# Layer norm's fold, its root from PSUM, the rounding of weights and the first maxima: an order changed in four places

## The reference, cut to what matters

```
# layer 0
p = rmsnorm(x, g_mix[0]) @ w_in_a            # 12 tiles of channels, and 2 of memory queries
v = a * sigmoid(gate)                        # u = p[:1536] + b_glu, split in two halves
v = causal_dwconv(v, w_dw_a, b_dw_a)         # 31 taps, 768 channels
v = silu(layernorm(v, ln_g, ln_b))           # over the 768 channels
x = x + concat(v, memory_attention(q, mem_k, mem_v)) @ w_out[0]
x = x + conv_ffn(rmsnorm(x, g_ffn[0]), ...)  # 5632 wide, 3 taps, silu(gate) * val
# layer 1
kvf = rmsnorm(x, g_kv) @ w_kvf               # keys, values, 12 forget gates
cum_logf = cumsum(log_sigmoid(f_logit + b_f))
q, q_mem = rmsnorm(x, g_mix[1]) @ w_in_b
x = x + concat(forgetting_attention(q, k, v, cum_logf), memory_attention(...)) @ w_out[1]
x = x + conv_ffn(rmsnorm(x, g_ffn[1]), ...)
```

## Time and profile before

| | us |
|---|---|
| median of 3 runs | 1698.44 |
| lowest and highest run | 1695.33, 1699.03 |
| profiled execution, its own time | 1693.87 |
| span of the profiled execution | 1692.0 |

### The profile page before, as it was taken

How to read it: one execution, slowest core, us unless ns; L and a number is a source line. 1 busy time by engine, 2 the same in 40 slices (tenths; PEclk the granted TensorE clock), 3 DMA queues, 4 the chain that set the end, 5 groups by cost and what they waited for, 6 DMA issues and landing times.

```text
span 1692.0 us, 23831 instructions
## 1 busy us (share of the span) xinstructions
PE 1647.4 (97%) x8600; PEld 1273.5 (75%) x8600; DVE 849.4 (50%) x1408; ACT 734.5 (43%) x1165; POOL 706.7 (42%) x406
## 2 busy tenths in 40 slices
PE   7899899999999999999999999999999999999998
PEld 7655678888888876666788888888876668876666
DVE  7787545555531125433466666511355554566454
ACT  6433434444432335444445555433335643525541
POOL 4433244444455444443444444545434432434332
PEclk9999999999999999999999999999999999999999
DMA  7112132233333332110223233333321112321111
GB/s 255 60 51 64 51 100 81 93 99 99 99 111 100 100 99 75 51 50 26 100 88 92 94 99 99 112 104 107 131 63 52 62 62 63 119 63 63 51 50 62
DMA packets 40250, 143.76 MB, mean 85 GB/s; under 512 B 4592, under 2 KB 4592, under 8 KB 40176
## 3 DMA queue, kind: packets, MB, share of 16 engines
q1 hardware_dynamic: 39168, 139.59, 25.9%
q10 hardware_dynamic: 1008, 3.15, 0.6%
HBM read 140.62 MB, written 2.10 MB: 84 GB/s over the span
## 4 chain that ended last, share of the span: by engine, by line
PE 88%; DVE 6%; ACT 2%; issue 1%; DMA 1%; SPq 0%; POOL 0%; DVEq 0%; ACTq 0%; POOLq 0%
PE banks L1715 23%; PE banks L1717 23%; PE banks L1716 23%; PE banks L1893 3%; PE banks L1911 3%; PE banks L1928 3%; PE banks L1761 2%; PE banks L1763 2%; PE banks L1762 2%; DVE chain L1381 1%; PE banks L1981 1%; DVE xs_lo L1176 1%; DMA raw<-wstream 1%; ACT prob L726 1%; DVE banks L1381 1%
## 5 line engine op out<-in xcount | busy, mean ns | idle before, releaser
L581 POOL TENSOR_TENSOR w_lo<-raw,w_hi 128x1024 fp32r<-128x1024 f32 x252 | 610.2, 2430 | 733.1 <-ACT w_hi L664 732.8
L1715 PE MATMUL banks<-xs_hi,w_hi 128*128 128x512 f32 (+2 forms) x1488 | 597.4, 401 | 11.3 <-DVE xs_lo L1432 4.7
L1717 PE MATMUL banks<-xs_hi,w_lo 128*128 128x512 f32 (+2 forms) x1488 | 577.9, 388 | 0.0
L1716 PE MATMUL banks<-xs_lo,w_hi 128*128 128x512 f32 (+2 forms) x1488 | 577.0, 388 | 0.0
L664 ACT ACTIVATE w_hi<-raw 128x1024 fp32r<-128x1024 f32 x255 | 264.0, 1053 | 287.6 <-PE banks L1717 247.2
L1715 PEld LDWEIGHTS banks<-xs_hi,w_hi 128*128 128x128 f32 x1488 | 280.3, 188 | 83.7 <-issue 18.3
L1717 PEld LDWEIGHTS banks<-xs_hi,w_lo 128*128 128x128 f32 x1488 | 279.8, 188 | 58.5
L1716 PEld LDWEIGHTS banks<-xs_lo,w_hi 128*128 128x128 f32 x1488 | 280.6, 189 | 53.6 <-issue 2.9
L591 POOL TENSOR_SCALAR prob<-prob,rinv 128x512 f32<-128x512 f32 (+3 forms) x144 | 89.3, 632 | 194.4 <-DVE rinv L1230 194.1
L1715 PE MATMUL banks<-hid_hi,w_hi 128*128 128x512 f32 x352 | 136.9, 389 | 0.0
L1716 PE MATMUL banks<-hid_lo,w_hi 128*128 128x512 f32 x352 | 136.9, 389 | 0.0
(11 more groups left out here) (258 smaller groups left out, 1935.6 us busy)
## 6 DMA issues: line engine op xcount, KB each, us to landing
raw<-wstream SPq DMA_DIRECT2D x255, 512.0 KB, 3.5
x<-xT SPq DMA_DIRECT2D x4, 512.0 KB, 10.2
out<-pt SPq DMA_DIRECT2D x8, 256.0 KB, 2.1
memx<-memT SPq DMA_DIRECT2D x2, 512.0 KB, 5.9
ws_sb<-wsT ACTq DMA_DIRECT2D x2, 512.0 KB, 4.5
qk<-post_rows ACTq DMA_DIRECT2D x2, 512.0 KB, 3.5
sb_sb<-sbT ACTq DMA_DIRECT2D x2, 256.0 KB, 5.0
rope_sb<-rope ACTq DMA_DIRECT2D x1, 512.0 KB, 6.5
```

The lines of the kernel that those rows point to most:

```text
L581: nc.gpsimd.tensor_tensor(w_lo[s][:].rearrange("p k c -> p (k c)"), raw[s][:], w_hi[s][:].rearrange("p k c -> p (k c)").bitcast(f32), SUB) ...
L1715: MM(dst, w_hi[slot][:, k, :], hi, start=start, stop=False)
L1716: MM(dst, w_hi[slot][:, k, :], lo, start=False, stop=False)
L1717: return MM(dst, w_lo[slot][:, k, :], hi, start=False, stop=stop)
```

## The change

It moves work in four places and drops one copy; no arithmetic is changed.

- **First attention blocks.** DVE's maxima of blocks 0 and 4 go ahead of the gate product of units 2 and 4; ACT's exponentials of block 0 go ahead of the first sigmoid.
- **Layer norm.** DVE takes five of the last tile's seven taps, finishes tile 4, and then takes the other two. PE's fold of the last tile goes ahead of the second memory unit, the last tile's sums into its middle, the total to step 1 of the third unit; ACT copies the sums down ahead of rounding a weight unit. The transposes that spread the root go ahead of the fourth output part, and DVE multiplies by the root in PSUM, without `spread`; the last product signals `cast_down` in its place.
- **Rounding of weights.** In `residual` the unit that was rounded ahead of the splits of x is rounded behind them, once DVE has written all low parts. At unit 8 of layer 1 the rounding waits for the low parts too.
- **Gates of layer 1.** `gate_sums` is cut in two: `gate_logs` (three instructions) stays where it was, and the scan with what follows goes behind block 7's maxima.

```diff
--- before.py
+++ after.py
@@ -691,10 +691,10 @@
                 else:
                     act.wait_ge(unit_used, last_unit + 1)
 
-            def residual(first, name, gain, change):
+            def residual(first, name, no, gain, change):
 
                 for m in range(KT):
-                    if first + m != U_OUT0:
+                    if first + m != U_OUT0 and m < KT - 1:
                         high_for(first + m)
                     if m == KT - 1:
                         for k in range(KT - 1):
@@ -703,6 +703,8 @@
                     act.wait_ge(acc_free, accs_before(first + m) + 1)
                     square(name, m, x[:, m, :])
                 A(xs_hi[:, KT - 1, :], x[:, KT - 1, :], ACT.Copy, scale=col(gain, KT - 1)).then_inc(split_hi, 1)
+                act.wait_ge(split_lo, KT * (no + 1))
+                high_for(first + KT - 1)
 
             def attend(a, hook):
                 pairs = a.heads // 2
@@ -839,13 +841,15 @@
                 if j == 1:
                     for t in range(2):
                         mem_values_down(t)
+                if j == 2:
+                    exponentials(att_m0, 0)
                 if j >= 2 and j % 2 == 0:
                     gate_sigmoid(j // 2 - 1)
                 if 7 <= j < 12:
                     parts_down(j - 7)
                 for k in range(KT):
                     for i in a_steps(j, k):
-                        if i < att_m0.n:
+                        if 0 < i < att_m0.n:
                             exponentials(att_m0, i)
                         if 1 <= i <= att_m0.n:
                             odd_down(att_m0, i - 1)
@@ -857,9 +861,9 @@
                 A(xs_hi[:, p, :], qm0[:, p, :], ACT.Copy).then_inc(split_hi, 1)
             high_for(U_MEM1 + 1)
             parts_down(MT - 1)
-            high_for(U_MEM1 + 2)
             act.wait_ge(ln_rows_up, 1)
             A(chan_sum[:], bank[2][:], ACT.Copy).then_inc(ln_rows_down, 1)
+            high_for(U_MEM1 + 2)
             for t in range(MT):
                 act.wait_ge(s_cent, t + 1)
                 A(glu[:, t, 0:T], conv[:, t, :], ACT.Square).then_inc(ln_squared, 1)
@@ -869,12 +873,15 @@
             A(rstd_ln[:], bank[4][:], ACT.Copy).then_inc(ln_rows_down, 1)
             high_for(U_OUT0)
             for t in range(MT):
-                act.wait_ge(s_norm, t + 1)
+                if t < MT - 1:
+                    act.wait_ge(s_norm, t + 1)
+                else:
+                    act.wait_ge(cast_down, cast_no["ln"] + 1)
                 own.link(A(conv[:, t, :], conv[:, t, :], ACT.Silu, scale=col("ln_g", t), bias=col("ln_b", t)))
                 if t == 0:
                     act.wait_ge(unit_used, U_MEM1)
                 A(xs_hi[:, 2 + t, :], conv[:, t, :], ACT.Copy).then_inc(split_hi, 1)
-            residual(U_OUT0, "f0", "g_ffn0", XF_O0)
+            residual(U_OUT0, "f0", SP_F0, "g_ffn0", XF_O0)
             ffn(0, U_UP0, U_DN0, "b")
 
 
@@ -896,6 +903,8 @@
                 A(xs_hi[:, 2 + p, :], att_f.o[0][:], ACT.Copy).then_inc(split_hi, 1)
 
             for j in range(B_UNITS):
+                if j == F_UNIT:
+                    act.wait_ge(split_lo, KT * (SP_KV + 1))
                 high_for(U_B + j)
                 if j in (3, 4):
                     values_down(VT_M1 + j - 3, vm1[:, :, (j - 3) * P:(j - 2) * P],
@@ -928,7 +937,7 @@
             values_down(VT_F + t, vf[:, :, t * P:(t + 1) * P], b_mix[:].rearrange("p (q c) -> p q c", c=P))
             for p in (MT - 2, MT - 1):
                 y_high_late(p)
-            residual(U_OUT1, "f1", "g_ffn1", XF_O1)
+            residual(U_OUT1, "f1", SP_F1, "g_ffn1", XF_O1)
             act.wait_ge(g_in_ok, 1)
             ffn(1, U_UP1, U_DN1, "fin")
 
@@ -958,7 +967,7 @@
                 def token_norm():
                     for t in range(AT):
                         if t < AT - 1:
-                            act.wait_ge(s_norm, MT + (AT - 1) * l + t + 1)
+                            act.wait_ge(s_norm, MT - 1 + (AT - 1) * l + t + 1)
                         else:
                             act.wait_ge(cast_down, cast_no[f"ln{l}"] + 1)
                         A(va[:, t, :], va[:, t, :], ACT.Identity, scale=col(f"lna_g{l}", t),
@@ -1390,13 +1399,16 @@
 
             for j in range(2 * MT):
                 t = j // 2 - 1
+                ahead = a_steps(j, 0) + a_steps(j, 1) if j in (2, 4) else []
+                for i in ahead:
+                    maxima(att_m0, i)
                 if j >= 2 and j % 2 == 0:
                     own.wait()
                     glu_product(t)
                 for k in range(KT):
                     at = KT * (j % 2) + k
                     for i in a_steps(j, k):
-                        if i < att_m0.n:
+                        if i < att_m0.n and i not in ahead:
                             maxima(att_m0, i)
                         if 1 <= i <= att_m0.n:
                             even_down(att_m0, i - 1)
@@ -1413,8 +1425,9 @@
                        bank=bank[6] if j == 2 else None)
             glu_product(MT - 1)
             own.wait()
-            conv_taps(MT - 1, 0, DVE_TAPS[MT - 1])
+            conv_taps(MT - 1, 0, 5)
             conv_finish(MT - 2)
+            conv_taps(MT - 1, 5, DVE_TAPS[MT - 1])
             conv_finish(MT - 1)
             layer_norm("ln", (0,), conv, MT, bank[2], Q)
             for p in range(2):
@@ -1423,10 +1436,11 @@
             for j in range(4):
                 mem_down(mem_kv1, j, U_MEM1, acc[j // 2])
             invert("ln")
-            spread("ln", rstd)
+            dve.wait_ge(cast_up, cast_no["ln"] + 1)
             for t in range(MT + 2):
                 if t < MT:
-                    V.tensor_tensor(conv[:, t, :], conv[:, t, :], rstd[:], MUL).then_inc(s_norm, 1)
+                    ins = V.tensor_tensor(conv[:, t, :], conv[:, t, :], cast_bank("ln")[:], MUL)
+                    ins.then_inc(s_norm if t < MT - 1 else cast_down, 1)
                 if t >= 2:
                     dve.wait_ge(split_hi, KT * SP_YA + t + 1)
                     V.tensor_tensor(xs_lo[:, t, :], conv[:, t - 2, :], xs_hi[:, t, :].bitcast(f32),
@@ -1444,11 +1458,13 @@
                 V.scalar_tensor_tensor(out=xs_lo[:, k, :], in0=x[:, k, :], scalar=col("g_kv", k),
                                        in1=xs_hi[:, k, :].bitcast(f32), op0=MUL, op1=SUB).then_inc(split_lo, 1)
 
-            def gate_sums():
+            def gate_logs():
                 dve.wait_ge(f_act, 3)
                 own.link(V.tensor_scalar(fl[2][:], fl[0][:], col("b_f"), 0.0, ADD, ALU.min))
                 own.link(V.tensor_tensor(fl[0][:], fl[1][:], fl[2][:], SUB))
                 own.link(V.memset(fl[2][:], 1.0))
+
+            def gate_sums():
                 own.link(V.tensor_tensor_scan(fl[3][:], fl[2][:], fl[0][:], 0.0, MUL, ADD))
                 own.link(V.tensor_copy(gates[:], fl[3][:]))
                 for low in (slice(P // 4, P // 2), slice(3 * P // 4, P)):
@@ -1468,10 +1484,12 @@
 
             for j in range(B_UNITS):
                 if j == F_UNIT + 2:
-                    gate_sums()
+                    gate_logs()
                 for k in range(KT):
                     for i in b_steps(j, k):
                         maxima(*b_block(i))
+                        if j == F_UNIT + 2:
+                            gate_sums()
                         late = b_pair(i)
                         if i and late is None:
                             even_down(*b_block(i - 1))
@@ -2095,10 +2113,10 @@
             mem_unit(U_MEM1, half_bank(acc[0], 0))
             conv_parts(MT - 1)
             ln_sums(0, MT - 1)
-            mem_unit(U_MEM1 + 1, half_bank(acc[0], 1))
             conv_fold(MT - 1)
-            ln_sums(MT - 1, MT).then_inc(ln_rows_up, 1)
-            mem_unit(U_MEM1 + 2, half_bank(acc[1], 0), before=[(3, ln_total)])
+            mem_unit(U_MEM1 + 1, half_bank(acc[0], 1),
+                     before=[(4, lambda: ln_sums(MT - 1, MT).then_inc(ln_rows_up, 1))])
+            mem_unit(U_MEM1 + 2, half_bank(acc[1], 0), before=[(1, ln_total)])
             mem_unit(U_MEM1 + 3, half_bank(acc[1], 1), before=[(4, lambda: ln_squares(0, NQ))])
             ln_squares(NQ, MT).then_inc(ln_rows_up, 1)
             out0_part(0, 0, 2)
@@ -2106,8 +2124,8 @@
             out0_part(1, 0, 2)
             pe.wait_ge(acc_free, U_OUT0)
             out0_part(2, 0, 2)
+            cast("ln")
             out0_part(3, 0, 2)
-            cast("ln")
             for m in range(NQ):
                 out0_part(m, 2, KT)
             for m in range(NQ, KT):
```

## The result

The changed kernel takes 1682.08 us, median of 4 (1681.77 to 1683.57), against 1698.11 us, median of 4 (1695.33 to 1699.03), in the same comparison: ratio 0.9914, 95% interval 0.99 to 0.9928. It is 16 us faster by the medians. Run once more beside other kernels it took 1682.04 us (1681.51 to 1683.04, 5 runs; ratio 0.9917, 0.9905 to 0.993). All nine executions have a mean granted clock of 0.997.

The account below looks back on a forecast made before the run. TensorE, busy 1647.4 of 1692.0 us, was taken as the bound, so only its waits could be won. Terms 0.7 + 4.7 + 2.95 + 1.9 = 10.25 us gave 1683.6 profiled, 1688.2 median with 4.6 added; range 1684 to 1693.

Parts of the forecast that it names:

- with the same distance, 1688.2: Final step: profiled execution foreseen at 1683.6 us, plus the 4.6 us between the earlier profiled execution and the median.
- Rival 2: Gain lost to clock 0.5 behind new waits and in the blocks among the gates: about 1692.5 us, 10%.
- up to the gates' wait at 85 us: First attention blocks among the gates: block 4 gains 0.93 us, block 0 loses 0.2; sum 0.7 (0.3 to 1.2).
- layer norm: Layer norm ahead of the output projection: shorter waits, earlier root, no copy; gain 4.7 us (3.0 to 5.5).
- first FFN's splits: Splits of x in both residual stages, one term: waits on low parts go, gain 2.95 us (2.0 to 3.0).
- middle layer: Key and value split gains 0.97 us, maxima ahead of the gates' scan 0.95; sum 1.9 us.
- the wait left: PE's wait ahead of the first output part with a normed tile: about 1.7 us instead of 3.75.
- Block 0: First attention block: moving its maxima and exponentials forward only moves PE's wait behind scores 1, a loss of 0.2 us.
- scores 1 without a wait: Sign in the changed profile: no wait at scores 1, one of about 2.9 us ahead of the transposes behind them.
- no table load: Assumed no extra 1.28 us load ahead of block 0's exponentials; with one, block 0 would come to -0.5 us.
- Rivals 1, 3 and 4: Layer norm catches elsewhere, about 1692, 14%; deferred roundings late, about 1703, 2%; time unchanged, within 3.4 us of 1698.4, 5%.
- no wait of PE on w_lo or w_hi stands in the FFNs: Sign: such waits at the third unit of either FFN would prove the prediction wrong.

Follow-up runs that it names:

- before_again: The unchanged kernel before, profiled a second time to look at a longer execution; that execution took 1698.89 us.
- p_mid: Kernel before with only the middle layer's changes (rounding behind the key and value split, gate sums behind the maxima): 1693.6 us, ratio 0.9984.
- s_f0_old: Changed kernel with the last weight rounding ahead of the splits of x again, for the first feed-forward only: 1688.39 us, ratio 0.9951 to the kernel before.
- q_copy: Changed kernel with the copy of the layer norm's root from PSUM to SBUF kept: 1682.51 us.
- q_norm_late: Changed kernel with the spreading of the layer norm's root behind the fourth output part again: 1683.07 us.
- p_round: Kernel before with only the rounding moved behind the splits of x in the two residual stages: 1691.07 us, ratio 0.9965.
- p_gates: Kernel before with only the maxima and exponentials of the first attention blocks moved: 1694.21 us, ratio 0.9981.
- s_j4: Changed kernel with only block 4's maxima behind the gate product of unit 4 again: 1683.65 us.
- s_j2: Changed kernel with only block 0's maxima and exponentials behind the gate product of unit 2 again: 1681.09 us, ratio 0.9894 to the kernel before.

## Why the prediction was wrong

**The step that failed is "with the same distance, 1688.2".** The sum was made against a profiled execution of 1693.87 us and the 4.6 us up to the median were carried over as if they were noise. They were not: in before_again they are matmuls at 1.2 GHz behind the waits of 1.77 and 2.16 us, worth 3.2 and 1.2 us, and the profiled execution had neither. By the clock, 29 of 57 executions are of the long kind; two long ones were profiled, one of this kernel (before_again) and one of p_mid, and s_f0_old brings the long ones back with the 1.8 us wait. The change takes the first wait away and halves the second, and the distance shrank to nothing. The profile was foreseen at 1683.6 and came to 1682.24, and the 4.6 became -0.2: of the 6.1 us by which the forecast was off, 4.7 are this step and 1.4 the sum. Rival 2 had the mechanism, and with the wrong sign: it asked which new wait would bring the slow clock, not which old one had it. A slow stretch does follow the new wait at 54 (clock 0.50 in 56 to 58), but the kernel before had one there already (0.52 in 54 to 56, behind its wait of 2.21 at 52.6), so nothing was lost by it.

**The sum, term by term**, each taken from one of PE's rows to the next in the second run of the changed kernel, against the first profile: up to the gates' wait at 85 us 0.5 (predicted 0.7; executions of one kernel differ by 0.7 there); layer norm 4.8 (4.7); first FFN's splits 3.2 and the second's 1.2, 4.3 together (2.95); middle layer 2.7 (1.9). These make 12.35 and the span moved by 12.3. (In the first profile of the changed kernel PE's first wait was 9.7 us instead of 8.2 and the attention rows came 0.8 later, so its 11.6 is less than the terms make.) The layer norm, the largest term, is right in its parts too: q_copy 0.73 for 0.7, q_norm_late 1.40 for 1.4, the wait left 1.62 for "about 1.7". The splits and the middle layer were mis-sized in the same way: a wait was priced at its recorded idle time. In the earlier trace rows that is counted from the modelled end of the last matmul, 0.40 us behind its start, while the next would have come 0.23 behind it; and the first matmul after a wait is followed at 0.33. That makes 0.27 more for each of the seven waits of these two terms, 1.9 us, nearly all of what was missing in them (2.15); p_round's 4.3, p_mid's 2.7 and s_f0_old's 0.26 for each wait agree.

**Block 0.** The step that it only moves PE's wait was right (scores 1 without a wait, 2.52 ahead of the transposes for "about 2.9"), and no table load stands ahead of its exponentials. Its price was too small: 0.3 us at the wait near 85 and 0.4 in the span by the profiles, 1.0 by medians of two chips, for 0.2.

**Rivals 1, 3 and 4** did not come. No unit's rounding was late: no wait of PE on w_lo or w_hi stands in the FFNs.

## What to carry to other kernels

Before a profile's own time is carried over to a median, ask what the executions differ by: profile a long one too, and look at the clock behind each wait that lies ahead of unhidden matmuls. Price a removed wait of PE at its idle time plus the restart, and look on both sides at which waits draw slow matmuls. When a wait comes back one step later each time that it is moved, the bound is the engine that feeds both steps, and its order is not the lever.

## What was not expected of the hardware

The same wait of 1.77 us was followed by some 6.8 us at half the clock in one execution and by none in another, with the same instructions. What decides it is open. p_gates kept that wait and has no execution above 1695.42, where the kernel before reaches 1700.28; s_f0_old has the shorter wait at 73 as well, and four of its six are long; and s_j4 had its slow stretches at other places than the wait that it restored. In s_j2 the stretch behind the layer norm is gone (clock 1.00 in 190 to 200) and one behind the wait at 84.67 has come (0.50 in 88 to 90). So a stretch doesn't hang on its own wait alone.
